# Last mixer of a two-block network: the convolution's transposes reordered, its centre tap on ScalarE, gates and squares issued earlier

## The reference

```python
def centred_short_conv(x, w):                       # w: 3 taps per channel
    xp = jnp.pad(x, ((0, 0), (1, 1), (0, 0)))
    return jax.nn.silu(sum(xp[:, tap:tap + T] * w[tap] for tap in range(3)))

def dn_inputs(pq, pk, pv, pa, pb):
    q_d, k_d, v_d = jnp.split(centred_short_conv(concat(pq, pk, pv), conv_w), 3, axis=-1)
    q_d = l2_normalize(heads(q_d)) * DN_HEAD_DIM ** -0.5     # x * rsqrt(sum(x*x) + EPS)
    k_d = l2_normalize(heads(k_d))
    beta = sigmoid(pb)
    g = -exp(a_log) * softplus(pa + dt_bias)
    return q_d, k_d, v_d, g, beta
# gated delta rule, in chunks of 64 tokens: G = cumsum(g), decays exp(G_i - G_j), exp(G), exp(G_last - G)
```

## Time and profile before

| what | value |
|---|---|
| median of three runs | 2013.8 us |
| profiled execution, its own time | 2020.15 us |
| its span | 2018.4 us |
| TensorE busy | 1896.1 us (94%) |
| VectorE busy | 1323.0 us (66%) |
| ScalarE busy | 975.7 us (48%) |
| mean granted TensorE clock | 0.979 of full |

### The profile page before, as it was taken

How to read it: one execution, slowest core, us unless ns; L and a number is a source line. 1 busy time by engine, 2 the same in 40 slices (tenths; PEclk the granted TensorE clock), 3 DMA queues, 4 the chain that set the end, 5 groups by cost and what they waited for, 6 DMA issues and landing times.

```text
span 2018.4 us, 32130 instructions
## 1 busy us (share of the span) xinstructions
PE 1896.1 (94%) x12994; PEld 1479.4 (73%) x12994; DVE 1323.0 (66%) x1603; ACT 975.7 (48%) x1657; POOL 112.6 (6%) x139
## 2 busy tenths in 40 slices
PE   3999999999999998999999999999999888799999
PEld 3777888655688864688877777877777677677887
DVE  5886776464688835588855589975437644366564
ACT  3567554333655434655456665446335332446553
POOL 1001000120100010100000010002000302000000
PEclk9999999999999999999999999998979999999999
DMA  8774887454599931499943368974123000234552
GB/s 324 280 260 145 298 297 283 164 199 161 195 345 329 355 112 63 167 344 330 353 140 126 126 222 289 356 271 158 60 70 124 2 4 4 101 112 159 178 186 104
DMA packets 215399, 393.30 MB, mean 195 GB/s; under 512 B 11337, under 2 KB 130133, under 8 KB 199893
## 3 DMA queue, kind: packets, MB, share of 16 engines
q1 hardware_dynamic: 214741, 391.12, 55.3%
q0 software_dynamic: 512, 0.13, 0.0%
HBM read 390.17 MB, written 1.05 MB: 194 GB/s over the span
## 4 chain that ended last, share of the span: by engine, by line
PE 84%; DVE 7%; ACT 5%; issue 3%; DMA 1%; POOL 0%; DVEq 0%; ACTq 0%; POOLq 0%
PE G L2196 19%; PE G L2197 19%; PE G L2201 19%; PE G L2439 4%; PE G L2550 2%; PE A L2288 2%; ACT full L1067 2%; DVE acc L1528 1%; PE G L2453 1%; DVE Z L2000 1%; PE G L2889 1%; PE A L2585 1%; PE A L2865 1%; PE A L2349 1%; DVE w_lo L1506 1%
## 5 line engine op out<-in xcount | busy, mean ns | idle before, releaser
L1506 DVE TENSOR_TENSOR w_lo<-raw,w_hi 128x1024 fp32r<-128x1024 f32 x452 | 536.1, 1209 | 205.5 <-ACT w_hi L977 196.8
L977 ACT CAST w_hi<-raw 128x1024 fp32r<-128x1024 f32 x452 | 461.7, 1040 | 431.3 <-PE G L2201 329.0
L2196 PE MATMUL G<-w_hi,h_hi 128*128 128x512 f32 (+2 forms) x1232 | 493.5, 401 | 14.3 <-ACT h_hi L1009 8.7
L2197 PE MATMUL G<-w_lo,h_hi 128*128 128x512 f32 (+2 forms) x1232 | 483.2, 393 | 0.0
L2201 PE MATMUL G<-w_hi,h_lo 128*128 128x512 f32 (+2 forms) x1232 | 382.2, 392 | 1.2 <-DVE h_lo L1545 1.2
L1528 DVE SCALAR_TENSOR_TENSOR acc<-raw,c_col,acc 128x2048 f32<-128x2048 f32 x120 | 282.1, 2351 | 28.7 <-DMA raw<-in_ada_w 17.6
L2196 PEld LDWEIGHTS G<-w_hi,h_hi 128*128 128x128 f32 x1232 | 236.5, 192 | 69.4 <-issue 19.4
L2201 PEld LDWEIGHTS G<-w_hi,h_lo 128*128 128x128 f32 x1232 | 234.6, 192 | 51.8 <-DVE h_lo L1545 2.5
L2197 PEld LDWEIGHTS G<-w_lo,h_hi 128*128 128x128 f32 x1232 | 236.9, 192 | 44.7
L2196 PE MATMUL G<-w_hi,act_hi 128*128 128x512 f32 (+2 forms) x640 | 254.6, 398 | 8.2 <-DVE w_lo L1506 3.1
L2197 PE MATMUL G<-w_lo,act_hi 128*128 128x512 f32 (+2 forms) x640 | 249.7, 391 | 0.0
(11 more groups left out here) (398 smaller groups left out, 1952.1 us busy)
## 6 DMA issues: line engine op xcount, KB each, us to landing
raw<-in_ada_w SPq DMA_DIRECT2D x96, 1024.0 KB, 6.0
raw<-in_ffn_w_gate SPq DMA_DIRECT2D x88, 512.0 KB, 3.9
raw<-in_ffn_w_up SPq DMA_DIRECT2D x88, 512.0 KB, 5.0
raw<-in_ffn_w_down SPq DMA_DIRECT2D x40, 1024.0 KB, 7.4
raw<-in_w_mlp SPq DMA_DIRECT2D x32, 1024.0 KB, 5.0
raw<-in_w_ada SPq DMA_DIRECT2D x24, 1024.0 KB, 6.7
raw<-in_w_in SPq DMA_DIRECT2D x18, 1024.0 KB, 5.1
raw<-in_sb_w_in SPq DMA_DIRECT2D x32, 512.0 KB, 5.2
```

The source lines that it names most:

```text
L977: nc.scalar.copy(w_hi[:, hc % (2 * HALVES), :, 0:n], landed_half(slot, j)[:, :, 0:n]).then_inc(hi_ready, 1)
L1506: nc.vector.tensor_tensor(w_lo_half, landed_half(slot, j)[:, :, 0:n], w_hi_half.bitcast(F32), ALU.subtract).then_inc(lo_ready, 1)
L2196: nc.tensor.matmul(bank, x_hi[:, kt, ts], w_hi[:, at, i, 0:n], start=first and i == 0, stop=False)
L2197: nc.tensor.matmul(bank, x_hi[:, kt, ts], w_lo[:, at, i, 0:n], start=False, stop=False)
```

## The change

The slot table is written anew and the steps are cut differently.

- In slots 15 to 18, X of the next tensor now stands ahead of Y of the present one, on all three engines.
- The centre tap of X moves from VectorE (4 instructions, line 1974 before) to ScalarE (4 activations of kind Copy with a per-partition scale), and VectorE's two other taps wait for it (`centre_ready`).
- Step L is cut into G (gates, slot 13), E (sums of the decay logarithms and their exponentials, slot 14), Q (one square each, slots 15, 17 and 19), R (its sum by head, slots 16, 18 and 20), and the remaining L (reciprocal root and products, slot 20). The load of ScalarE's table set with exp and ln moves behind the last Silu, in slot 19.
- TensorE's sums of E go to bank A1 alone, and TensorE's waits are changed to match.

The diff, cut to its core:

```diff
-                     8: [("P", 1)], 8.5: [("V", 1), ("S", 2)], 10: [("P", 2)], 11: [("V", 2), ("S", 3)], 13: [("P", 3)],
-                     14: [("V", 3), ("X", 0)], 15: [("Y", 0), ("X", 1)], 16: [("Y", 1), ("X", 2)], 17: [("Y", 2), ("X", 3)],
-                     18: [("Y", 3), ("X", 4)], 19: [("Y", 4)], 20: [("L", 0)], 21: [("W", 0)]}
+                     8: [("P", 1)], 8.5: [("V", 1), ("S", 2)], 10: [("P", 2)], 11: [("V", 2), ("S", 3)], 13: [("P", 3), ("G", 0)],
+                     14: [("E", 0), ("V", 3), ("X", 0)], 15: [("X", 1), ("Y", 0), ("Q", 0)], 16: [("X", 2), ("Y", 1), ("R", 0)],
+                     17: [("X", 3), ("Y", 2), ("Q", 1)], 18: [("X", 4), ("Y", 3), ("R", 1)], 19: [("Y", 4), ("Q", 2)], 20: [("R", 2), ("L", 0)], 21: [("W", 0)]}
...
 # ScalarE, step X
+                    act.wait_ge(cvT_done, s + 1)
+                    if s >= 2:
+                        act.wait_ge(cvB_done, s - 1)
+                    for a in range(4):
+                        c = NCOL + 12 + 4 * CONV[s][1] + a
+                        ins = nc.scalar.activation(conv_t[:, s % 2, a], A[2 * ((s + 1) % 2) + a // 2][:, SEQ * (a % 2):SEQ * (a % 2) + SEQ], ACT.Copy, scale=cols[:, c:c + 1])
+                    ins.then_inc(centre_ready, 1)
                 elif step == "Y":
                     act.wait_ge(conv_ready, s + 1)
                     nc.scalar.activation(conv_t[:, s % 2], conv_t[:, s % 2], ACT.Silu).then_inc(cs_ready, 1)
+                    if s == 4:
+                        nc.scalar.preload_act_table_set("natural_log_exp_and_others")
                     act.wait_ge(cvB_done, s + 1)
...
 # VectorE, step X
-                    dve.wait_ge(cvT_done, s + 1)
-                    if s >= 2:
-                        dve.wait_ge(cvB_done, s - 1)
-                    for tap, (lo, hi) in ((1, (0, SEQ)), (0, (1, SEQ)), (2, (0, SEQ - 1))):
+                    dve.wait_ge(centre_ready, s + 1)
+                    for tap, (lo, hi) in ((0, (1, SEQ)), (2, (0, SEQ - 1))):
...
 # TensorE
                 elif step == "X":
                     x = CONV[s][0]
-                    if s:
+                    if s == 1:
                         pe.wait_ge(split_full, k.f)
+                        pe.wait_ge(eg_ready, 1)
...
-                elif step == "L":
-
-                    pe.wait_ge(cb_ready, 5)
+                elif step == "E":
+
+                    pe.wait_ge(waT_act, 8)
+                    pe.wait_ge(waT_dve, 8)
                     pe.wait_ge(gates_ready, 1)
                     pe.wait_ge(delta_in, 16)
...
                 elif step == "W":
-                    pe.wait_ge(eg_ready, 1)
+                    pe.wait_ge(cb_ready, 5)
```

More of the change, by code:

```diff
@@ L360, in build @@
         gl_ready = sem("gl_ready")
-        ea_ready = sem("ea_ready")
+        centre_ready = sem("centre_ready")
         gates_ready = sem("gates_ready")
@@ L1332, in lat_step @@
                     ins.then_inc(cb_ready, 1)
-                elif step == "L":
-                    nc.scalar.preload_act_table_set("natural_log_exp_and_others")
+                elif step == "G":
                     act.wait_ge(gz_ready, 1)
@@ L1895, in head_norm, with delta_gates @@
                 ins.then_inc(qk_ready, 1)
-            def delta_inputs():
+            def delta_gates():
                 dve.wait_ge(free_act, k.free_act)
@@ L1910, in delta_inputs, with gate_sums, square_sums @@
                 nc.vector.tensor_scalar(lnb_all, gate_s[:, :, 16:32], -1.0, None, ALU.mult).then_inc(gates_ready, 1)
[L1911 to L1914, removed]
+            def gate_sums():
+                dve.wait_ge(gates_ready, 1)
+                dve.wait_ge(eg_ready, 1)
+                dve.wait_ge(beta_ready, 1)
+                for d in range(2):
+                    nc.vector.tensor_tensor(lnb_G[:, d], lnb_all[:, :, DNH * d:DNH * d + DNH], neg_G[:, d], ALU.subtract)
+                for d in range(2):
+                    ins = nc.vector.scalar_tensor_tensor(out=beG[:, d], in0=beta[:, :, d], scalar=-1.0, in1=e_G[:, d], op0=ALU.mult, op1=ALU.mult)
+                ins.then_inc(beg_ready, 1)
+            def square_sums(i):
+                dve.wait_ge(l2q_ready, i + 1)
+                nc.vector.tensor_reduce(ss16[:, 16 * i:16 * i + 16].rearrange("p (t h) -> p t h", t=NT),
+                                        sq_t[i % 2].rearrange("p t (h d) -> p t h d", d=HD), AX.X, ALU.add).then_inc(l2s_ready, 1)
+            def delta_inputs():
                 dve.wait_ge(l2s_ready, 3)
@@ L1922, in delta_inputs @@
                     ins.then_inc(l2_ready, 1)
-                dve.wait_ge(eg_ready, 1)
-                dve.wait_ge(beta_ready, 1)
-                for d in range(2):
-                    nc.vector.tensor_tensor(lnb_G[:, d], lnb_all[:, :, DNH * d:DNH * d + DNH], neg_G[:, d], ALU.subtract)
-                for d in range(2):
-                    ins = nc.vector.scalar_tensor_tensor(out=beG[:, d], in0=beta[:, :, d], scalar=-1.0, in1=e_G[:, d], op0=ALU.mult, op1=ALU.mult)
-                ins.then_inc(beg_ready, 1)
             def lat_step(step, s):
@@ L1972, in lat_step @@
                             y, col = conv_t[:, s % 2, a, lo:hi], cols[:, c:c + 1]
[L1973 to L1976, removed]
+                            ins = nc.vector.scalar_tensor_tensor(out=y, in0=src, scalar=col, in1=y, op0=ALU.mult, op1=ALU.add)
                         if tap < 2:
@@ L1979, in lat_step @@
                     ins.then_inc(conv_ready, 1)
+                elif step == "G":
+                    delta_gates()
+                elif step == "E":
+                    gate_sums()
+                elif step == "R":
+                    square_sums(s)
                 elif step == "L":
@@ L2687, in lat_step @@
                         for i, m_ in enumerate((tri_dir, later_dir)):
-                            nc.tensor.matmul(A[0][:, 64 * i + 32 * d:64 * i + 32 * d + 32].rearrange("p (s h) -> p s h", s=4), m_[:, d],
+                            nc.tensor.matmul(A[1][:, 64 * i + 32 * d:64 * i + 32 * d + 32].rearrange("p (s h) -> p s h", s=4), m_[:, d],
                                              g_all[:, :, 8 * d:8 * d + 8], start=True, stop=True)
@@ L2692, in lat_step @@
                                 c = 2 * rd + st
-                                ins = nc.tensor.matmul(A[1][CH * d:CH * d + CH, 8 * c:8 * c + 8], half[:, st if d == 0 else 1 - st],
+                                ins = nc.tensor.matmul(A[1][CH * d:CH * d + CH, 128 + 8 * c:136 + 8 * c], half[:, st if d == 0 else 1 - st],
                                                        g_all[:, delta_tile(rd, d)[1], 8 * d:8 * d + 8], start=True, stop=True)
```

26 lines of the change are left out of this document (13 added, 13 removed).

## The result

The changed kernel took 2031.58 us in the median of 8 runs (2021.14 to 2034.86), the kernel before 2019.85 us in the median of 8 runs (2013.56 to 2027.33; the three runs that the prediction knew are among them). The ratio is 1.0055, 95% interval 1.0033 to 1.0077, which is 6.7 to 15.5 us slower. In a second series (12 runs of the change, 35 of the kernel before) the ratio was 1.0040 (1.0020 to 1.0059). The forecast was 8.0 us slower; its absolute time, 2022 us with a range of 2012 to 2029, was missed. The prediction took 20 us for the least that a measurement of this kernel can tell from no change; these intervals are about 4 us to either side.

A forecast was written before the change was run, and what follows sets the result against it. The prediction took the kernel to be bound by TensorE, busy for 94% of the span. Its terms, 3.2 + 7.8 - 0.8 - 5.3 + 3.1, summed to +8.0 us on a median of 2013.8: 2022 us, range 2012 to 2029.

The forecast's parts named there:

- the last one of the sum: Whole kernel: adding +8.0 us to the earlier runs' median of 2013.8 us gives 2022 us.
- slots 15 to 18: TensorE waits for centre tap and Silu on ScalarE; four slots at 10.2 us instead of 32.90 in all: +7.8 us.
- one fall at 3.1: Slot 14 to step W: one new fall of TensorE's clock, out of six possible places, costing +3.1 us.
- slot 14, the sums: The 40 small matmuls of the decay sums, moved behind unit 14, lie on TensorE's path at full clock: +3.2 us.
- slot 19: The last Silu is ready before its unit ends, so the slot takes 6.50 us instead of 7.32: -0.8 us.
- unit 20 to the delta rule: From unit 20's start to the delta rule's first product, 18.6 us instead of 23.97: -5.3 us.
- The centre tap: Four activations on ScalarE, between 1.15 and 1.94 us together, taken as 1.55 us.
- The waits: TensorE's idle time ahead of the transposes back, in four slots, grows from 0.73 to about 2.6 us.
- Step W: Ahead of the delta rule, the query's transposes wait about 3 us for VectorE's copy of the context key.
- The rival with a fall at every stall: Clock falls at four idle times, slot 14's sums and step W, 3.1 us each: +23.5, 2037 us; chance 7%.
- The rival in which the loop opens up: ScalarE doesn't hold TensorE, so waits in slots 15 to 18 vanish: -9.3, 2004.5 us; chance 10%.
- the old fall: Slot 20 before the change: clock fell behind 2.16 us idle and the 40 small matmuls, costing 3.1 us.

The follow-up runs named there:

- the Silu first: The change with ScalarE's Silu of tensor s ahead of the centre tap of tensor s+1; ratio 0.9993 to the kernel before.
- The two kernels with W first: The change with step W's copies ahead of VectorE's subtraction, plus Silu ahead of the next centre tap (ratio 0.9981) or centre tap on VectorE (0.9964).
- the centre tap on VectorE with W first: The change with the centre tap back on VectorE and step W's copies ahead of VectorE's subtraction in slot 21; 2010.62 us, ratio 0.9964.

## Why the prediction was wrong, by its own steps

**The step that failed is the last one of the sum**: "it was 6.3 us above the median of the runs, a difference that this change doesn't touch, so the median of 2013.8 becomes 2022 us". The +8.0 us was added to a median of three runs, two of them at 2013.6 and 2013.8 and one at 2027.3. That median was a low draw: later ones of the same kernel were 2019.85 (8 runs, those three among them), 2017.78 and 2018.82 (35 each) and 2018.86 (12). The difference of 6 us to the profiled execution was in plain sight. The measured 2031.58 lies 9.8 us above 2013.8 + 8.0: 6.1 of them are the base (2019.85 against 2013.8) and 3.7 the difference (11.7 between the medians against 8.0). On a base of 2019.85 the forecast reads 2027.9 and its range, moved by the same 6 us, 2018 to 2035, which takes in the measured time. The range had taken in the bounds of the unknown costs and no bound at all for the base. The sign and the size of the difference were right: +8.0 lies in both intervals (6.7 to 15.5 us, and 4.0 to 11.9).

In the pair of profiles the stretch grew by 6.1 us, 1.9 less than the sum: 0.5 by the sums, 0.5 by slots 15 to 18 without their fall, 0.9 by the clock, with two terms of under 0.2 against each other. That the clock came so near is luck: one fall at 3.1 was a choice between 0 and 18.6, and what came were two falls at 2.2 together, and three in the second profile.

**Term by term**, in the first profile of the change:

| term | forecast | measured |
|---|---|---|
| slot 14, the sums | +3.2 | 11.96 - 9.29 = +2.7 |
| slots 15 to 18 | +7.8 | 41.85 - 32.90 = +9.0, of it 1.6 by a fall of the clock |
| slot 19 | -0.8 | 6.37 - 7.32 = -0.95 |
| unit 20 to the delta rule | -5.3 | 19.44 - 23.97 = -4.5, of it +0.6 by a fall |
| behind the stretch | (in the clock term) | 425.5 - 425.2 = +0.3 |

*The centre tap* was bounded at 1.15 and 1.94 us and put at 1.55; it took 1.57. By the formula of the Trainium skill, "ScalarE: Activation LUTs", section "What ACT_TABLE_LOAD costs", it would have been 1.69 as an estimate; the nearest rows of the trace came closer.

*The waits* came at 2.60 to 2.61 us where 2.6 was said, at slots of 10.06 and 10.07 us at full clock where 10.2 was said. That they are due to ScalarE's order is shown: with the Silu first, or with no centre tap on ScalarE, they go, while the order of TensorE's transposes stays.

*Step W* waits 3.07 us for the copy of the context key; about 3 was said. That the subtraction makes it is shown by putting it behind the copies: 0.80.

*The sums* took 1531.81 to about 1535 us at full clock. Only 2.7 us came on top of slot 14, since the first of the attention's products starts at 1534.58, while the last of the sums run.

*The clock.* I had taken one fall of 3.1 us net. The first profile of the change had two in the stretch, the second three, against one in the kernel before. The fall behind the sums in the second profile cost slot 14 1.66 us (13.62 against 11.96 us), half of the price that I had used; it lasted 3.4 us, the old one 6.8. The one behind the first wait cost 1.6. The one in step W cost 0.6 in the stretch and reached into the delta rule: from its first product to its first product with `LT` the change takes 1617.21 - 1605.88 = 11.3 us, the kernel before 1603.05 - 1593.17 = 9.9. Part of these 1.4 us is won back at once, since TensorE's next wait, for VectorE's `LT`, is 0.16 us instead of 0.85, and by the end of the program 0.3 are left. In the second pair of profiles the part behind the stretch is 2.1 us longer (425.3 against 423.2), so the price there is not settled. The rival with a fall at every stall was wrong: of eight waits of 2.6 us in the two profiles, two were followed by one, in each profile the first of the four.

*The rival in which the loop opens up* was wrong for this change. The two kernels with W first go its way, with 5.3 and 5.7 us less than the 73.5 us of before where it had 9.3; each has one fall of the clock in the stretch, behind the sums.

## What to carry to other kernels

When a step is put ahead on one engine to hide a latency, walk the same order on every other in-order engine: a link that is taken off a covered path can land on ScalarE between two neighbouring steps of TensorE, and here 2.5 us uncovered cost more than 5 us under a unit. What TensorE waits for should be issued ahead of a prefetch on the engine that makes it; here one subtraction in the wrong place cost some 3 us, 0.6 of them by the clock. And add a forecast difference to a base with a spread of its own: where three runs lie 14 us apart, and the profile 6 us from their median, the base is less certain than the sum.

## What the runs showed of the hardware

The 40 small matmuls of the decay sums can be followed by a fall of the clock without any idle time ahead of them. In five of the seven profiles with them in slot 14 the granted clock went to 0.50 during or just behind them; in none of the three profiles without them did it fall in that slot. One such case, the centre tap on VectorE with W first (TensorE by stretches), the sums first and the attention's products next:

```profile
1537.00:1540.00 3.00, 3.00 (x40) 1.00 0.00 0
1541.00:1544.00 3.00, 3.00 (x13) 0.52 0.87 317
```

In the prediction I had put the old fall down to the idle time and the sums together; the sums can do it without the idle time. In step W the clock fell within the wait of 3.07 us in all five profiles that have it, and in neither of the two with a wait of 0.80. Of the eight waits of 2.6 us two were followed by a fall, and of the 18 waits of 0.73 to 0.90 us ahead of transposes back, in the four profiles with the old order, none.

The Trainium skill ("TensorE: Matmul & The Clock Gate", section "A second HAM failure mode: psum-queue depth-cycling") tells of a kernel in which small idle times between groups of matmuls make the clock swing. The traces agree for the waits of 3.07 us, only sometimes for those of 2.6, and not for those under 1. What decides in the single case was not tried.

The same kernel scatters over 23 us (2006.84 to 2029.73 in 35 runs), and in the ten profiles the start of unit 14 goes with the time that TensorE spends at half clock ahead of it. Why that time differs from run to run stays open.
